# Two feed-forward loops written out over a ring of weight tiles, and two small reads moved between the feed-forwards

## The reference, cut to what matters

```python
for i in range(2):
    u = rmsnorm(h, norm_mix[i])
    h = h + (dsw_mixer if i == 0 else moba_mixer)(u, ...)   # attention; a q,k,v product first
    h = h + sq_relu_mlp(rmsnorm(h, norm_ffn[i]), ffn_w1[i], ffn_w2[i])

def sq_relu_mlp(h, w1, w2):        # w1 is 1024 x 4096, w2 is 4096 x 1024
    return jnp.square(jax.nn.relu(h @ w1)) @ w2
```

```python
mod  = silu(c)     @ mod_w[i] + mod_b[i]     # 6144 values: six rows of shift, scale, gate
modc = silu(c_ctx) @ mod_w[i] + mod_b[i]     # the same for the context
hx = rmsnorm(x, ln1_g[i]) * (1 + sc1) + sh1  # and so on
```

## Time and profile before

| what | value |
|---|---|
| timed runs | 2465.33 us median (2458.99 to 2465.79) |
| profiled execution, its own time | 2459.23 us |
| its span in the trace | 2457.4 us |
| mean granted TensorE clock | 0.928 |
| PE busy | 2099.8 us (85%) |
| DVE busy | 766.9 us (31%) |
| ACT busy | 360.7 us (15%) |
| POOL busy | 186.4 us (8%) |
| HBM read, written | 625.47 MB, 26.57 MB |

### The profile page before, as it was taken

The page is one execution under the profiler, slowest core; times in us unless marked ns, Lnnn a source line. Parts: engine busy times, 40 slices in busy tenths (PEclk is TensorE's granted clock), DMA queues, the critical chain, the costliest instruction groups (busy, mean ns, idle before and its releaser), DMA issues.

```text
span 2457.4 us, 22294 instructions
## 1 busy us (share of the span) xinstructions
PE 2099.8 (85%) x8645; PEld 1096.0 (45%) x8645; DVE 766.9 (31%) x1684; ACT 360.7 (15%) x775; POOL 186.4 (8%) x225
## 2 busy tenths in 40 slices
PE   7998989898898999878698888888487799888884
PEld 3456656444565666334443333333254433333332
DVE  1236573114659225952311110111343311111111
ACT  2231000123100121431100000000232100000000
POOL 0000000000000000000011111111000011111100
PEclk9999999998999999999699989999799699999997
DMA  9832688342459612002299999999632399999994
GB/s 253 296 133 80 237 322 304 122 150 73 176 185 375 232 57 96 42 18 88 82 407 410 400 414 408 398 411 409 249 152 88 132 417 421 418 409 417 406 409 180
DMA packets 128050, 631.46 MB, mean 257 GB/s; under 512 B 14263, under 2 KB 16471, under 8 KB 102129
## 3 DMA queue, kind: packets, MB, share of 16 engines
q1 hardware_dynamic: 109056, 592.94, 61.1%
q0 software_dynamic: 17744, 34.33, 5.1%
q10 hardware_dynamic: 1184, 3.35, 0.4%
HBM read 625.47 MB, written 26.57 MB: 265 GB/s over the span
## 4 chain that ended last, share of the span: by engine, by line
DMA 24%; PE 21%; DVE 3%; issue 2%; ACT 1%; SPq 0%; POOLq 0%; POOL 0%; DVEq 0%; ACTq 0%
DMA ring<-ex_up 23%; PE PS L1027 14%; PE PS L1045 2%; PE PS L438 2%; PE PS L716 1%; PE PS L1018 1%; DMA arena<-rows_d 1%; PE PS L1036 1%; SPq L1630 0%; ACT arena L629 0%; PE PS L1030 0%; PE PS L338 0%; DVE arena L1341 0%; DVE arena L1343 0%; DMA arena<-tokens_d,arena 0%
## 5 line engine op out<-in xcount | busy, mean ns | idle before, releaser
L1027 PE MATMUL PS<-ring,arena 128*64 128x512 f32 x1040 | 518.7, 657 | 114.9 <-DMA ring<-ex_up 112.8
L1030 PE MATMUL PS<-ring,arena 128*64 128x512 f32 x1040 | 519.2, 657 | 0.0
L1027 PEld LDWEIGHTS PS<-ring,arena 128*64 128x64 f32 x1040 | 150.8, 151 | 418.9 <-issue 375.8
L438 PE MATMUL PS<-ring,arena 128*128 128x512 f32 (+1 forms) x736 | 300.0, 563 | 8.4 <-issue 5.4
L1310 DVE COPY arena<-PS 128x512 f32<-128x512 f32 x64 | 44.3, 692 | 671.2 <-PE PS L1018 671.2
L1045 PE MATMUL PS<-ring,arena 128*64 128x512 f32 x1040 | 237.4, 598 | 1.5 <-DVE arena L1306 1.5
L768 PE MATMUL PS<-ring,arena 128*128 128x512 f32 x512 | 225.9, 600 | 13.6 <-DVE arena L840 13.6
L757 PE MATMUL PS<-arena,ring 128*128 128x256 f32 x1024 | 226.6, 383 | 2.2 <-issue 1.6
L757 PEld LDWEIGHTS PS<-arena,ring 128*128 128x128 f32 x1024 | 194.8, 191 | 38.8 <-issue 12.5
L438 PEld LDWEIGHTS PS<-ring,arena 128*128 128x128 f32 x736 | 139.1, 193 | 149.9 <-issue 140.4
L768 PEld LDWEIGHTS PS<-ring,arena 128*128 128x128 f32 x512 | 98.5, 193 | 132.4 <-issue 131.8
(11 more groups left out here) (229 smaller groups left out, 1659.1 us busy)
## 6 DMA issues: line engine op xcount, KB each, us to landing
ring<-ex_gate SPq DMA_DIRECT2D x65, 2048.0 KB, 17.8
ring<-ex_up SPq DMA_DIRECT2D x65, 2048.0 KB, 22.8
ring<-ex_down SPq DMA_DIRECT2D x65, 2048.0 KB, 23.7
ring<-ffn_w SPq DMA_DIRECT2D x32, 2048.0 KB, 12.5
ring<-mod_w SPq DMA_DIRECT2D x24, 2048.0 KB, 8.1
ring<-a_w_qkv SPq DMA_DIRECT2D x9, 2048.0 KB, 37.7
ring<-b_w_qkv SPq DMA_DIRECT2D x6, 2048.0 KB, 9.7
ring<-w_in_ab SPq DMA_DIRECT2D x3, 2048.0 KB, 9.1
```

The costliest lines, as they stand in the source:

```text
L438: mm = pe.matmul(PS[:, u % 4, 0:w.width], q.src[:, k, w.t * P:(w.t + 1) * P], w8(w.tile, w.width)[:, k, :], start=(k == 0), stop=(k == KD ...
L1027: g = pe.matmul(PS[0:CAP, u, :], xT[:, k, :], w8(gate)[:, k, :], start=(k == 0), stop=(k == KD - 1))
L1030: h = pe.matmul(PS[CAP:P, u, :], xT[:, k, :], w8(up)[:, k, :], start=(k == 0), stop=(k == KD - 1))
```

## The change: what it does

1. The body is 16 tiles handed out once, so the slots go round in order through both feed-forwards. On all engines that used the loop (PE and SP; ACT and DVE had their rounds written out already and only look up other tiles) the four body rounds are written out.
2. The rows of mod_d for layer 0 and conv_w are read by POOL as soon as A is done (it waits for mod_d's writes and for A's last addition), into `modacc`, which no round uses then, instead of into the arena. PE transposes them behind the transposes of the norm after A, into banks 6 and 7, in front of the q/k/v product; DVE copies them out behind its half of that norm.
3. The read of mod_d for layer 1 stays at its place and goes into `modacc` too.

```diff
@@ rings
-            body = R.tiles(8, trips=2)
+            body = R.tiles(16)
@@ pe_ffn
-            with pe.Fori(0, 2) as i:
-                for h in range(2):
-                    j = 2 * i + h + 1
-                    w1(T.body[4 * h], j + 1, i)
-                    w2(T.body[4 * h + 3], j, 1 - h, i)
-                    mod_sums(j, 1 - h, T.body[4 * h + 1:4 * h + 3], i)
+            for j in range(1, FF_TILES - 3):
+                first, mod_a, mod_b, second = T.body[4 * (j - 1):4 * j]
+                w1(first, j + 1)
+                w2(second, j, j % 2)
+                mod_sums(j, j % 2, (mod_a, mod_b), 0)
@@ buffers
-        modrows = area(7168, 2, P)
-        convrows = arena[0:TAPS, 14848:14848 + BANK]
+        modrows = modacc[:, 0, 0:2 * P].rearrange("p (a b) -> p a b", a=2)
+        convrows = modacc[0:TAPS, 1, :]
@@ sync, ffn_loads
-                with sp.Fori(0, 2) as i:
-                    for h in range(2):
-                        one_pass(T.body[4 * h:4 * h + 4], 2 * i + h + 1, i)
+                for r in range(1, MOD_N // 2 - 1):
+                    one_pass(T.body[4 * (r - 1):4 * r], r)
@@ tensor
             pe_norm(pe, n_b1)
+            turn_mod(0, 6)
+            pe.wait_ge(s_conv.w_rows, 16)
+            for c in range(4):
+                mm = pe.transpose(PS[:, 7, c * TAPS:(c + 1) * TAPS], convrows[:, c * P:(c + 1) * P],
+                                  ident[0:TAPS, 0:TAPS])
+            mm.then_inc(s_conv.w_turned, 1)
             at(pe, *n_b1.done)
             pe_qkv(pe, q_b)
...
             pe_norm(pe, n_b2)
-            turn_mod(0, 4)
-            pe.wait_ge(s_conv.w_rows, 16)
-            for c in range(4):
...
@@ vector
+            dve_norm(dve, n_b1)
+            modulation(0, 6)
             dve.wait_ge(s_conv.w_turned, 1)
...
+            dve_qkv(dve, q_b)
@@ gpsimd
             pool_ffn(pool, f_a)
+            at(pool, *f_a.mod_stored, *f_a.done)
+            mod_rows(0)
+            pool.dma_start(convrows, ins["conv_w_2"][0]).then_inc(s_conv.w_rows, 16)
             at(pool, *n_b1.done)
             bias_load_b(0)
...
             pool.dma_start(cx, ins["ctx_2"][0].rearrange("(t p) d -> p t d", p=P)).then_inc(s_cx, 16)
-            pool.dma_start(convrows, ins["conv_w_2"][0]).then_inc(s_conv.w_rows, 16)
...
-            at(pool, *f_a.mod_stored)
-            mod_rows(0)
             rope_loads(L0, "q_norm_a_2", "k_norm_a_2")
```

More of the change, by code:

```diff
@@ L809, in ffn_tile @@
                 return T.head[j], 0
-            return (T.body[4 * (j % 2)], (j - 2) // 2) if j < FF_TILES - 2 else (T.tail[4 * (j % 2)], 0)
+            return (T.body[4 * (j - 2)] if j < FF_TILES - 2 else T.tail[4 * (j % 2)]), 0
         def mod_tiles(T, r):
@@ L815, in mod_tiles @@
                 return T.head[2:4], 0
-            return (T.body[4 * ((r - 1) % 2) + 1:][:2], (r - 1) // 2) if r < MOD_N // 2 - 1 else (T.tail[1:3], 0)
+            return (T.body[4 * r - 3:4 * r - 1] if r < MOD_N // 2 - 1 else T.tail[1:3]), 0
         def act_ffn(act, f, tail=None):
@@ L1748, in _, with turn_mod @@
             pe_ffn(pe, f_a)
+            def turn_mod(l, bank):
+                pe.wait_ge(s_mod.rows, 16 * (l + 1))
+                pe.transpose(PS[:, bank, 0:96], modrows[0:96, l, :], ident[0:96, 0:96]).then_inc(s_mod.turned, 1)
             pe_norm(pe, n_b1)
+            turn_mod(0, 6)
[4 more added lines that the diff above has]
+            mm.then_inc(s_conv.w_turned, 1)
             at(pe, *n_b1.done)
@@ L1756, in _ @@
             L0, L1 = second
-            def turn_mod(l, bank):
-                pe.wait_ge(s_mod.rows, 16 * (l + 1))
-                pe.transpose(PS[:, bank, 0:96], modrows[0:96, l, :], ident[0:96, 0:96]).then_inc(s_mod.turned, 1)
-            turn_mod(0, 4)
-            pe.wait_ge(s_conv.w_rows, 16)
-            for c in range(4):
-                mm = pe.transpose(PS[:, 5, c * TAPS:(c + 1) * TAPS], convrows[:, c * P:(c + 1) * P],
-                                  ident[0:TAPS, 0:TAPS])
-            mm.then_inc(s_conv.w_turned, 1)
             def ctx_norm():
@@ L1985, in _ @@
             dve_ffn(dve, f_a)
[L1986 to L1991, removed]
             def modulation(l, bank):
@@ L2002, in modulation @@
                            .then_inc(s_mod.gain, 1)
-            modulation(0, 4)
+            dve_norm(dve, n_b1)
+            modulation(0, 6)
             dve.wait_ge(s_conv.w_turned, 1)
-            dve.tensor_copy(convw[:, :, :], PS[:, 5, 0:4 * TAPS].rearrange("p (c k) -> p c k", c=4))\
+            dve.tensor_copy(convw[:, :, :], PS[:, 7, 0:4 * TAPS].rearrange("p (c k) -> p c k", c=4))\
                .then_inc(s_conv.w_ready, 1)
+            dve_qkv(dve, q_b)
+            dve_pairs(dve, at_b)
+            dve_proj(dve, pr_b)
+            dve_norm(dve, n_b2)
+            L0, L1 = second
             def rope_tables(L):
@@ L2140, in _, with mod_rows @@
             pool_ffn(pool, f_a)
+            def mod_rows(l):
+                pool.dma_start(modrows[0:96, l, :], mod_d[l].rearrange("j (r c) -> (j r) c", c=P))\
+                    .then_inc(s_mod.rows, 16)
+            at(pool, *f_a.mod_stored, *f_a.done)
+            mod_rows(0)
+            pool.dma_start(convrows, ins["conv_w_2"][0]).then_inc(s_conv.w_rows, 16)
             at(pool, *n_b1.done)
@@ L2159, in _ @@
             pool.dma_start(cx, ins["ctx_2"][0].rearrange("(t p) d -> p t d", p=P)).then_inc(s_cx, 16)
-            pool.dma_start(convrows, ins["conv_w_2"][0]).then_inc(s_conv.w_rows, 16)
-            def mod_rows(l):
-                pool.dma_start(modrows[0:96, l, :], mod_d[l].rearrange("j (r c) -> (j r) c", c=P))\
-                    .then_inc(s_mod.rows, 16)
-            at(pool, *f_a.mod_stored)
-            mod_rows(0)
             rope_loads(L0, "q_norm_a_2", "k_norm_a_2")
```

## The result

The changed kernel takes 2440.67 us in the median of four runs (2432.66 to 2444.28), the kernel before 2463.15 us in four (2458.99 to 2465.79). The ratio is 0.9901, with a 95% interval of 0.9881 to 0.9921: by it 24.4 us less, 19.5 to 29.3, where the two medians lie 22.5 us apart. Two later repeats of the changed kernel gave 2434.30 and 2437.47 us; over all its 14 executions the median is 2437.5. Forecast were 2438 us and a gain of 24.3.

The account below looks back on a forecast made before the run. Bound by a chain of waits split between DMA (24%) and PE (21%), PE work ahead of 1211 us; 17.69 + 4.70 + 1.94 - 0 = 24.3 us off 2459.23 gives 2434.9, median put at 2438, range 2430 to 2450.

Parts of the forecast that it names:

- The fourth rounds: Round with w1(4), w2(3) in both feed-forwards: 37.47 us in A, 37.70 in B become 28.74, gaining 17.69 us.
- a landing: Mod_w tile mA(3) in the fourth round: issued at about 284.8, lands 8.1 us later at 292.9, before DVE is free.
- The slack: In the fourth round, hidden(3) is complete at 311.2 and PE wants it at 328.5: 17 us to spare.
- B behind its norm: Start of the second feed-forward: 0.05 us after its norm is ready, at 626.94 instead of 631.64, gaining 4.70 us.
- The clock at B: B's first 128 matmuls: 29.80 us falls to A's 27.86, gaining 1.94 us; bounds 0 and 1.94.
- The reads behind A: Before q/k/v: both reads land by about 459.5, transposes fit a 1.32 us gap, price 0; at worst 5.3 us.
- The level: Whole kernel: 2434.9 from the profiled execution, median put midway between 2434.9 and 2441, at 2438 us.
- The longer program: Feed-forward rounds: the loop's branches and the longer written-out program were put at nothing.
- The late reads: Rival before q/k/v: PE stands up to 5.3 us, giving 2443, or 2445 with half clock at B; chance 0.11.
- The moved stall: Rival in the feed-forward rounds: another wait replaces mA(3)'s, the 17.7 us are lost, giving 2459; chance 0.07.
- Slower expert stages: Rival in the two expert stages: engines write the shifted slots slower, 112 us more, giving 2550; chance 0.03.

Follow-up runs that it names:

- The ring alone: Kernel before with only the 16-tile slot order and written-out rounds, reads, transposes and copies as before: 2441.55 us, ratio 0.9922.
- the old slots: Changed kernel, rounds still written out, but the second eight body tiles in the same slots as the first eight: 2460.79 us, ratio 1.0001.
- one held load: Changed kernel, SP waits once more before loading mA(3): for w2(2) in the first feed-forward, w1(3) in the second: 2444.34 us, ratio 0.9932.
- the late-read run: Changed kernel, POOL issues the two reads behind the norm after the first feed-forward, some 7 us later: 2442.17 us, ratio 0.9909.
- the kernel with five added matmuls: Changed kernel plus five unread matmuls before the norm's transposes, before and behind A and before B: 2430.80 us, ratio 0.9879; with reads earlier 2430.78, 0.9882.
- the old ones: Kernel before, only rounds written out, slots kept: 2464.01 us, ratio 1.0011; changed kernel, second eight tiles in the first eight's slots: 2460.79 us, ratio 1.0001.

## Why the prediction was right

- **The fourth rounds** (17.69 us). Right: 8.73 and 8.96 us, exactly as reckoned, because the excess was read off one round against its neighbours. The ring alone gives it, the old slots take it back without a loop, and one held load makes half of it.
- **Inside that step, a landing was mis-sized.** I took 8.1 us for mA(3), the median of mod_w's landings, and had DVE find it there. DVE waited 2.05 us for it and took it at 300.04, 11.7 us after its issue. The two mod_w tiles of a round differ: mA(3) goes out while other tiles still come in (the DMA engines are at a share of 1.04 to 1.05 from 286 to 298 us), mB(3) finds them idle (0.00 from 302 to 304) and was taken 8.2 us after its issue. hidden(3) had 16.9 us of slack instead of 17.3, since it hangs on mB(3). The slack took the error.
- **B behind its norm** (4.70 us). Right in size: 4.76 in the trace. Two small errors cancel in it: B starts 0.26 us behind DVE's norm in place of 0.05, and the norm's transposes ran 0.20 us shorter than before (3.39 for 3.59).
- **The clock at B** (1.94 us). Right in size, and better founded than I put it. I called it a matter of luck. In three profiles with the reads in front of B the first product takes 29.80, 29.90 and 29.97 us; in the seven with the reads moved and no added matmuls it takes 27.86 or 27.87. At this place the clock went with the place of the reads in all ten. What differs there is PE's pause right before B, 4.18 to 4.55 us and the five small transposes against 1.53 to 1.74 us; no run parts the pause from the transposes. A short pause alone is no warrant: what was luck is the row I took as the model, A's 27.86, since in nine of the ten profiles without added matmuls A's first product takes 29.6 to 30.0 us behind a pause of only 1.37. The Trainium skill (TensorE: Matmul & The Clock Gate, "What's actually happening") lets the clock's change depend on a rhythm that the kernel does not set. q/k/v's first product behind A, 14.00, 14.00 and 15.47 us in the three profiles of the changed kernel, agrees with that; B's first product shows nothing of it.
- **The reads behind A** (0). Right: conv_w landed 5.0 us after its issue, between the bounds of 2.0 and 10.7, at 454.3, when PE was about done with the norm's transposes, and PE still had 0.60 us to spare before q/k/v. The Trainium skill's 2.0 us plus bytes (DMA: Bandwidth & Descriptors, the anatomy of one DMA on the gpsimd path) is what it took on idle queues in the late-read run, not here beside a 2 MB tile. POOL took 0.54 and 0.55 us for its two issues where I allowed 0.94. Nothing was lost, and issuing the reads earlier won nothing in the kernel with five added matmuls, where that was tried.
- **The level.** Partly luck. The sum gave 2434.9 from the profiled execution, and I added 3 us for two levels that I saw in four executions. The 45 further executions of the kernel before show no two levels: they spread from 2456.77 to 2468.83, with medians of 2460.58 to 2461.55, 1.4 to 2.3 us over the profiled execution. The changed kernel's 14 have a median of 2437.5 between 2429.66 and 2444.28; the six fastest have a mean clock of 0.931 to 0.935, the other eight 0.926 to 0.931.
- **The longer program** (0). I put the loop's branches and the longer program at nothing. With the new slots nothing speaks against it; with the old ones 2.7 and some 6 us appeared beside a lower mean clock, and that stays open.
- **The rivals.** The late reads: no wait of PE for them in the three traces of the changed kernel. The moved stall: out, by the ring alone. Slower expert stages: out, 386 to 388 GB/s in other slots.

## What to carry to other kernels

A loop keeps its tiles in the same slots in every trip. Where its body has 8 tiles and the ring 6 slots, the second trip starts in slots that were used last: its first two loads, w1(4) and mA(3), wait for a tile two back instead of six, and all behind them wait too. Either the body is written out, as here, or its number of tiles has to be a multiple of the ring's, which follows from the slot order and which no run here tried. The price is read directly as the excess of one round over its neighbours, with the slow clock behind the stall in it. A small read whose data is long complete belongs under an idle time that its consumer has anyway; a pause taken away from in front of a long product can give back its clock as well.

## What the runs showed of the hardware

- Behind PE's pauses of 4.6 to 5.1 us ahead of a norm the norm's transposes take 3.3 to 3.7 us in place of 1.91, at a granted clock of 0.50 to 0.58 (0.50 is 1.2 GHz), and often the first part of the next product runs at half clock too. At A the two go together: in nine profiles the transposes took 3.67 or 3.68 us and the product 29.6 to 30.0, in the tenth 3.30 and 27.86.
- Filling these pauses with 4.4 us of idle matmuls kept the clock at 1.00 at all three places in one profile, for 6.7 us by the medians and 3.2 by the ratios. In the second such profile q/k/v's first product still took 15.7 us.
- A float32 matmul of 128x512 shows as two records of 0.43 us at full clock: ten took 8.75 us.
- Executions of one and the same kernel differ by up to 15 us, and the mean granted clock roughly goes with it: 12 executions of the changed kernel with the old slots went from 2455.06 us at 0.930 to 2468.52 at 0.923. A part's worth below 5 us was only seen in the traces.
